# Fourteen matmuls on constants at the seam between two layers of a streaming-encoder trunk

## What is computed

```python
for i in range(DEPTH):
    h = rmsnorm(x, norm_mix[i])
    if i % N_MIXERS == 0:
        x = x + stick_breaking_mixer(h, sb_w_in[j], sb_w_out[j])
    else:
        x = x + mlstm_mixer(h, ml_w_in[j], ml_b_i[j], ml_b_f[j], ml_g_head[j], ml_w_out[j])
    h = rmsnorm(x, norm_ffn[i])
    x = x + hierarchical_moe(h, ...)     # 32 experts, 2 chosen per position
return rmsnorm(x, norm_final)
```

## Time and profile before

| | us |
|---|---|
| median of 3 runs | 1767.63 |
| lowest, highest | 1766.57, 1768.25 |
| the profiled execution | 1768.82 |
| its span, first to last instruction | 1767.1 |
| mean granted clock of TensorE | 0.946 |

### The profile page before, as it was taken

The page is one execution under the profiler, slowest core; times in us unless marked ns, Lnnn a source line. Parts: engine busy times, 40 slices in busy tenths (PEclk is TensorE's granted clock), DMA queues, the critical chain, the costliest instruction groups (busy, mean ns, idle before and its releaser), DMA issues.

```text
span 1767.1 us, 25607 instructions
## 1 busy us (share of the span) xinstructions
PE 1568.3 (89%) x9901; PEld 1074.5 (61%) x9901; DVE 729.4 (41%) x1167; ACT 423.4 (24%) x571; POOL 64.9 (4%) x90
## 2 busy tenths in 40 slices
PE   7999999999997788878799999999999887788775
PEld 7999999888543234423287988988864443243322
DVE  4454454443332222223264757657434232223223
ACT  5343443433000000000054334343320000000002
POOL 2210100100100000000011000000000000000000
PEclk9999999999998898889899999999999888998897
DMA  7645555578999999999954455566699999999996
GB/s 262 196 150 167 160 172 168 214 263 305 371 384 425 427 425 425 425 427 424 417 181 146 144 190 178 178 234 213 225 356 394 422 424 425 427 424 424 425 426 264
DMA packets 149643, 543.79 MB, mean 308 GB/s; under 512 B 8864, under 2 KB 25680, under 8 KB 116432
## 3 DMA queue, kind: packets, MB, share of 16 engines
q1 hardware_dynamic: 148448, 541.14, 78.8%
q0 software_dynamic: 1136, 1.82, 0.4%
HBM read 540.83 MB, written 2.10 MB: 307 GB/s over the span
## 4 chain that ended last, share of the span: by engine, by line
PE 58%; DMA 27%; issue 5%; SPq 5%; DVE 2%; ACT 2%; POOL 1%; POOLq 0%; DVEq 0%; ACTq 0%
PE psum_G L706 30%; DMA ring<-in_moe_w 26%; PE psum_S L706 16%; PE psum_A L706 7%; SPq L521 5%; PE psum_T L706 4%; DVE w_lo L421 1%; ACT w_hi L417 1%; ACT h L1365 0%; POOL arena L668 0%; ACT arena L1199 0%; PE psum_A L713 0%; DVE x L1710 0%; POOLq L642 0%; DVE h L1960 0%
## 5 line engine op out<-in xcount | busy, mean ns | idle before, releaser
L706 PE MATMUL psum_A<-ring,arena 128*32 128x512 f32 x2048 | 297.5, 711 | 146.3 <-DMA ring<-in_moe_w 142.5
L421 DVE TENSOR_TENSOR w_lo<-ring,w_hi 128x2048 fp32r<-128x2048 f32 x126 | 289.1, 2298 | 288.3 <-ACT w_hi L417 282.9
L417 ACT CAST w_hi<-ring 128x2048 fp32r<-128x2048 f32 x128 | 244.1, 1908 | 242.5 <-PE psum_G L706 154.3
L706 PEld LDWEIGHTS psum_A<-ring,arena 128*32 128x32 f32 x2048 | 68.5, 120 | 316.9 <-issue 315.1
L1843 DVE COPY arena_two<-psum_A 128x512 f32<-128x512 f32 x64 | 44.3, 692 | 382.6 <-PE psum_T L706 350.0
L1875 DVE TENSOR_TENSOR x<-x,psum_S 128x512 f32<-128x512 f32 x128 | 88.0, 688 | 168.7 <-PE psum_S L706 168.7
L706 PE MATMUL psum_G<-xT_hi,w_hi 128*128 128x256 f32 x512 | 148.7, 290 | 1.0 <-DVE w_lo L421 1.0
L706 PE MATMUL psum_G<-xT_hi,w_lo 128*128 128x256 f32 x512 | 144.8, 283 | 0.0
L706 PE MATMUL psum_G<-xT_lo,w_hi 128*128 128x256 f32 x512 | 144.7, 283 | 0.0
L706 PE MATMUL psum_G<-ring,arena_two 128*32 128x512 f32 x976 | 121.5, 618 | 16.1 <-DMA ring<-in_moe_w 16.0
L1381 ACT ACTIVATE arena_two<-psum_T 128x64 f32<-128x64 f32 x64 | 14.4, 224 | 488.6 <-PE psum_T L706 488.6
(11 more groups left out here) (239 smaller groups left out, 2124.0 us busy)
## 6 DMA issues: line engine op xcount, KB each, us to landing
ring<-in_moe_w SPq DMA_DIRECT2D x378, 1024.0 KB, 18.8
ring<-in_sb_w_in SPq DMA_DIRECT2D x48, 1024.0 KB, 5.0
ring<-in_ml_w_in SPq DMA_DIRECT2D x48, 1024.0 KB, 5.2
ring<-in_sb_w_out SPq DMA_DIRECT2D x16, 1024.0 KB, 4.9
ring<-in_ml_w_out SPq DMA_DIRECT2D x16, 1024.0 KB, 5.1
turned_slots<-in_moe_w SPq DMA_DIRECT2D x6, 1024.0 KB, 12.6
x<-in_x SPq DMA_DIRECT2D x2, 1024.0 KB, 6.0
out_x<-h SPq DMA_DIRECT2D x4, 512.0 KB, 2.8
```

Source lines behind the costliest of these rows:

```text
L417: act.copy(w_hi[:, slot_place(j), :], ring[:, slot_place(j), :]).then_inc(hi_made, 1)
L421: dve.tensor_tensor(w_lo[:, slot_place(j), :], ring[:, slot_place(j), :], w_hi[:, slot_place(j), :].bitcast(F32), ALU.subtract).then_inc(l ...
L706: return pe.matmul(dst, lhsT, rhs, start=start, stop=stop, skip_group_check=True)
```

## The change

TensorE calls `keep_busy("T1", 14)` in the second turn of its loop over the layers, behind layer 0's `overflow` and ahead of its wait for `x_final`. Nothing else is changed.

```diff
@@ -1179,6 +1179,7 @@
             for layer in (0, 1):
                 if layer:
+                    keep_busy("T1", 14)
                     pe.wait_ge(x_final, 1)
                 else:
                     for b in range(TB):
```

## The result

The kernel with the 14 matmuls took 1777.33 us (median of 6 runs, 1770.56 to 1781.28) against 1768.52 us of the kernel before (median of 6, 1766.57 to 1769.98). The ratio is 1.0045, with a 95% interval of 1.0029 to 1.0061. I had forecast slower, 1772.1 us, with a range of 1769.8 to 1774.0. The direction was right and the measured median lies 3.3 us above my range. The two lists already hint at the reason: the lowest times differ by 4.0 us, the highest by 11.3.

The account below looks back on a forecast made before the run. TensorE, busy 89% of the span, was taken as the bound, held at the seam by its branch; 4.72 us of passes less about 0.2 us gained gave +4.5 on 1767.63, so 1772.1 us, range 1769.8 to 1774.0.

Parts of the forecast that it names:

- The wait at the seam is the branch, not x: Between the layers, TensorE's overflow branch (3.847 us) holds it to 890.35, while x_final is set at 888.83.
- All of the passes are on the path: At the seam, 28 passes stand behind the branch, ahead of the first transpose, moving it by 4.72 us.
- The price of a pass: Each added matmul is two passes, 0.112 us a pass at 2.4 GHz, 0.213 us at 1.2 GHz.
- The clock under the passes: At the seam, passes run 1.39 us at full clock, then 3.33 us at half clock, 4.72 us in all.
- the other case: Passes at the seam keep full clock or the low stretch falls elsewhere: +2.9 us, 1770.5; chance 0.12.
- What the transposes gain: Layer 1's transposes run 1.7 us faster at full clock, but GpSimd's subtraction for slot 1 leaves about 0.2 us.
- The shift reaches the end: The 4.5 us delay at slot 1 passes through the mixer and DMA-bound experts of layer 1 to the end.
- The sum's base and the range: Whole kernel: 4.5 us added to the 1767.63 median gives 1772.1, range 1769.8 to 1774.0.
- The first: Rival: passes at the seam keep full clock or the low stretch falls elsewhere, +2.9 us, 1770.5; chance 0.12.
- The second (hidden): Rival: with a short branch at the seam the passes are hidden, slot 1 0.7 us earlier, 1766.9; chance 0.06.
- The third (given back by the experts): Rival: the seam pays but layer 1's DMA-bound experts give it back, 0 to +2 us; chance 0.09.
- The fourth (a further stall): Rival: new instructions at the seam stall again or all run at half clock, +5.8 to +8.4 us; chance 0.08.

Follow-up runs that it names:

- again: The changed kernel (14 matmuls at the seam) measured once more without edit, against the kernel before: 1773.0 us, ratio 1.0008.
- moved loads: Changed kernel (14 matmuls at the seam) with the eight gate-weight loads issued by ScalarE instead of GpSimd: 1770.93 us, ratio 1.0017 to the kernel before.
- VectorE's split: Kernel with gate loads on ScalarE and 14 matmuls at the seam, but VectorE instead of GpSimd splits layer 1's slot 1: 1770.47 us, ratio 1.0009.
- the shift alone: Kernel before with the 14 matmuls at the start of TensorE's program, moving later code by 56 instructions, none at the seam: 1769.4 us, ratio 1.0007.

## Why the prediction was right, and where it was wrong

**The wait at the seam is the branch, not x.** Right. In every profile with the matmuls directly behind a long branch the first pass follows the branch's end; where the branch was short the first pass started 1.8 us ahead of x_final.

**All of the passes are on the path.** Right. Behind the long branch 14 at the seam cost 2.5 to 4.5 us, 14 more another 3.3 to 4.9, the same 14 at TensorE's end nothing.

**The price of a pass.** Right: 28 passes took 3.12 us at 2.4 GHz (3.13 worked out) and 4.75 us with a low stretch on them (4.72 worked out).

**The clock under the passes.** Half right. I took it from one trace and gave the other case 0.12. Of five profiles with 14 matmuls right behind a long branch, four had full clock (first measurement, again, moved loads, VectorE's split) and one the low stretch. In the two profiles with 28 matmuls the low stretch began 4.75 and 3.0 us after the last addition, so within the first 14 matmuls or ahead of them, which makes it three of seven. Full clock should have had far more than 0.12. The difference of 4.4 us in the means is nearer the low case, and its interval of 3.3 to 5.4 leaves out 2.85 us, but not a mixture such as four of seven at 2.85 and three at 4.45 (3.5 us). How often each occurs in the unprofiled runs stays open; the profiles are too few, and that 4.4 comes so near my 4.5 does not confirm the clock that I had assumed.

**What the transposes gain.** Right in kind. TensorE waits 1.0 us at slot 1 (1.2 forecast) and with VectorE's split that wait is gone. Faster transposes are worth 0.2 us against the trace that I worked from, as forecast, and 0.7 us where the low stretch lay on the first ones, not 1.7.

**The shift reaches the end.** Right: 2.7 us behind the last addition against 2.49 at the seam, and layer 1's experts last 451.7 us against 451.5. One reading on the way was wrong without changing anything: of the nine rows of TensorE's waits between 896 and 1376 two are "issue", so it waits for another engine or a DMA in seven places, not nine.

**The sum's base and the range.** This is the step that failed. I set the sum against the median of three runs within 1.7 us of each other and allowed for nothing in layer 0, since the change is behind it. So a term of the sum stood at nothing that measured 8.4 us in the profiled execution of the changed kernel, against 2.5 us at the seam. And it is no effect of the change alone: in 99 runs of the kernel before 21 lie above 1772 (up to 1778.41) and 78 below. The trace of before had the cause in it: VectorE's 4.2 us wait for gate_b, behind a row of small loads whose gaps on GpSimd vary from 1.9 to 5.3 us. I had not read that part because the change doesn't touch it. A wait that ends on something as loose as that, with nothing slack behind it, belongs in the range. The first measurement of the changed kernel had three of six runs near 1780, which are most likely late executions plus the seam (the one of them that was profiled is); in all 18 runs five lie above 1776. All runs together, 18 of the changed kernel and 99 of the one before, have medians of 1773.7 and 1768.9, +4.8 us (2.9 to 6.5 by drawing the lists again), near the 4.5 that I forecast for the difference. That agreement is worth little, because the share of late runs differs between the series: above 1774 lie 0 of 6, 13 of 35, 2 of 31 and 4 of 27 runs of the kernel before, and the last three series ran on three chips. The 4.4 us of the kernels with moved loads (3.3 to 5.4) is the better measure. That six runs held three late ones, beside none of six of the kernel before, I put down to chance; nothing here shows that the change makes them more frequent, and 18 runs can't exclude it.

**The rivals.** The first occurred in four of five profiles. The second (hidden) came out nearly as priced under its condition, a short branch, though 1.1 us of the passes still stood on the path. The third (given back by the experts) is refuted: nothing was given back. The fourth (a further stall) did not occur.

## What to carry to other kernels

Before work is put into a gap to keep an engine busy, read what ends the gap on that engine's own sequencer: here it was the engine's branch, not the semaphore behind it, so matmuls on constants placed behind it were all on the path. Placed ahead of it, the same ones left the time of the kernel before unchanged, but part of that was a shorter branch behind shifted code: at the seam they took 0.6 us more than the shift alone. A faster clock for the work that follows is worth only the slack to the next chain (0.2 us of 1.7 in the trace before). And look for waits that end on loosely timed small loads in stages that the change doesn't touch: they decide how many runs a median needs.

## What the runs showed of the hardware

The time of a branch over a long body that isn't run depended on the position of the code. On TensorE at the seam it was 3.3 to 3.9 us in ten profiles without added code ahead of it and 0.45 to 1.7 us in the four with 56 instructions ahead, the source being the same; on VectorE and ScalarE it was 0.05 to 0.06 us. Position is not the whole of it: with the same TensorE program it took 1.67 us in one kernel and 0.45 us in another. The Trainium skill, Runtime: NRT & Kernel Launch, section Instruction fetch mechanics, says that instructions come in blocks and that a branch out of the blocks at hand has to wait. The position dependence fits that; no run here shows the fetch itself.

A granted clock of 1.2 GHz after 3.1 to 3.7 us of idle time at the seam came in five of ten profiles and not in the others (and in one of two after 2.0 us), and it began 2.7 to 5.0 us after the start of the last addition where it came. One trace doesn't tell whether a gap of that length costs a low-clock stretch.

Small loads issued by GpSimd drifted by up to 10.7 us between executions (last one issued between 81.6 and 92.3 us). With eight of them moved to ScalarE's queue 11 runs spread over 3.8 us, where 31 runs of the kernel before beside them spread over 11.1.
